# A two-block layer on one core: three norms split into halves, the residual into quarters, the last FFN tiles ahead of the last down blocks

## The reference, cut to what matters

```python
x = x + 0.5 * rmsnorm(swiglu(rmsnorm(x, ffn1_pre_g), w_gu, w_down), ffn1_post_g)
h = rmsnorm(x, mix_pre_g); ...                      # attention + state space, then w_mix_out
x = x + rmsnorm(mixed, mix_post_g)
qx = rmsnorm(x, xa_pre_g) @ xa_w_q                  # norm 3 of the kernel
kx, vx = split(rmsnorm(mem, mem_norm_g) @ xa_w_kv)  # norm 1
x = x + rmsnorm(softmax(qx kx) vx @ xa_w_o, xa_post_g)
x = x + 0.5 * rmsnorm(swiglu(rmsnorm(x, ffn2_pre_g), ...), ffn2_post_g)   # norm 4
proj = rms_norm(x, g_norm_2) @ w_in_2; ...          # norm 5, second block
```

## Time and profile before

| | |
|---|---|
| median of 3 runs | 1121.4 us (1121.01 to 1122.61) |
| the profiled execution | 1121.69 us, of which the span is 1119.9 us |
| PE busy | 1104.4 us, 99% of the span, 8484 matmul records |
| DVE busy | 793.0 us, 71% |
| ACT busy | 590.9 us, 53% |
| DMA | 188.59 MB, mean 168 GB/s |

### The profile page before, as it was taken

One profiled execution on the slowest core, in us unless ns is written; L12 is line 12 of the kernel. 1 busy time (PEld: TensorE's weight loads), 2 busy tenths in 40 slices (PEclk: granted clock), 3 DMA queues, 4 the chain that ended last, 5 costly groups with the idle time before them and its releaser, 6 DMA issues.

```text
span 1119.9 us, 20894 instructions
## 1 busy us (share of the span) xinstructions
PE 1104.4 (99%) x8484; PEld 1042.5 (93%) x8484; DVE 793.0 (71%) x1112; ACT 590.9 (53%) x844; POOL 0.2 (0%) x4
## 2 busy tenths in 40 slices
PE   9999999999999999999999999999999999999998
PEld 8999999999999999999999898999999799999998
DVE  5755555858898977777777867665555686987774
ACT  5444444557664325586744555443443575664561
POOL 0000000000000000000000000000000000000000
PEclk9999999999999999999999999999999999999999
DMA  8665555455544236444555434355555345543341
GB/s 298 241 222 187 190 184 188 168 183 180 185 151 148 94 136 207 155 147 151 188 174 177 169 114 160 131 200 206 173 176 206 128 166 198 184 151 114 114 151 38
DMA packets 29137, 188.59 MB, mean 168 GB/s; under 512 B 3496, under 2 KB 4809, under 8 KB 7370
## 3 DMA queue, kind: packets, MB, share of 16 engines
q1 hardware_dynamic: 26592, 181.42, 46.8%
q10 hardware_dynamic: 2474, 6.15, 1.7%
HBM read 186.50 MB, written 1.05 MB: 167 GB/s over the span
## 4 chain that ended last, share of the span: by engine, by line
PE 79%; DVE 15%; ACT 4%; issue 2%; DVEq 0%; ACTq 0%
PE bank L500 23%; PE bank L502 23%; PE bank L501 23%; DVE sb_w_lo L1973 4%; PE bank L581 2%; DVE sb_ssd_conv L2196 1%; ACT sb_w_hi L1287 1%; PE bank L816 1%; PE bank L961 1%; PE bank L655 1%; PE bank L1033 0%; PE bank L1012 0%; DVE sb_ssd_xdt L2243 0%; DVE sb_hyF L2626 0%; DVE sb_hyF L2625 0%
## 5 line engine op out<-in xcount | busy, mean ns | idle before, releaser
L1973 DVE TENSOR_TENSOR sb_w_lo<-sb_w_raw,sb_w_hi 128x2048 fp32r<-128x2048 f32 x169 | 386.5, 2290 | 156.9 <-ACT sb_w_hi L1287 156.7
L500 PE MATMUL bank<-sb_hT_hi,sb_w_hi 128*128 128x256 f32 x1560 | 442.7, 284 | 1.4 <-DVE sb_hT_lo L2050 1.3
L502 PE MATMUL bank<-sb_hT_hi,sb_w_lo 128*128 128x256 f32 x1560 | 435.3, 279 | 0.0
L501 PE MATMUL bank<-sb_hT_lo,sb_w_hi 128*128 128x256 f32 x1560 | 435.2, 279 | 0.0
L1287 ACT ACTIVATE sb_w_hi<-sb_w_raw 128x2048 fp32r<-128x2048 f32 x169 | 322.4, 1908 | 36.3 <-PE bank L502 34.9
L500 PEld LDWEIGHTS bank<-sb_hT_hi,sb_w_hi 128*128 128x128 f32 x1560 | 292.2, 187 | 6.0 <-issue 3.6
L501 PEld LDWEIGHTS bank<-sb_hT_lo,sb_w_hi 128*128 128x128 f32 x1560 | 291.8, 187 | 2.4 <-issue 1.2
L502 PEld LDWEIGHTS bank<-sb_hT_hi,sb_w_lo 128*128 128x128 f32 x1560 | 292.3, 187 | 0.0
L1341 ACT ACTIVATE sb_ffn_gate<-sb_ffn_gate 128x256 f32<-128x256 f32 x44 | 18.4, 418 | 140.7 <-DVE sb_ffn_gate L2065 140.7
L500 PE MATMUL bank<-sb_w_hi,sb_hT_hi 128*128 128x256 f32 x256 | 73.2, 286 | 0.6 <-DVE sb_hT_lo L2725 0.3
L501 PE MATMUL bank<-sb_w_lo,sb_hT_hi 128*128 128x256 f32 x256 | 71.1, 278 | 0.0
(11 more groups left out here) (431 smaller groups left out, 1751.3 us busy)
## 6 DMA issues: line engine op xcount, KB each, us to landing
sb_w_raw<-in_w SPq DMA_DIRECT2D x169, 1024.0 KB, 5.0
sb_x<-in_x SPq DMA_DIRECT2D x2, 512.0 KB, 4.6
sb_w_raw<-in_w SPq DMA_DIRECT2D x4, 256.0 KB, 7.0
sb_w_raw<-in_w SPq DMA_DIRECT2D x2, 512.0 KB, 8.2
sb_mem_xn<-in_mem ACTq DMA_DIRECT2D x1, 1024.0 KB, 7.8
sb_post_g<-in_ffn_post_g ACTq DMA_DIRECT2D x2, 512.0 KB, 4.6
sb_decay<-in_c_decay ACTq DMA_DIRECT2D x1, 768.0 KB, 4.3
out<-sb_x SPq DMA_DIRECT2D x3, 256.0 KB, 2.2
```

Of the source, the lines that this page charges most:

```text
L500: pe.matmul(o, a_hi, b_hi, start=first, stop=False)
L501: pe.matmul(o, a_hi, b_lo, start=False, stop=False)
L502: return pe.matmul(o, a_lo, b_hi, start=False, stop=last)
L1973: tt(w_lo[b % STAGES][:], w_raw[b % RING][:], f32(w_hi[b % STAGES][:]), ALU.subtract).then_inc(w_lo_in, 1)
```

## The change

Six edits.

1. **Norms 3, 4 and 5 in halves.** `raw_turn` transposes only columns 0 to 511 of x (banks 3, 4) ahead of the first block; the other eight transposes stand inside that block, in front of k = 4. The block (`raw_feature`, `raw_token`) has its two output tiles in two banks (7 and b % 3) and runs all products with the high halves of x first (k = 0 to 7, four each), then those with the low halves (two per k).
2. **Residual in quarters.** x is added to in four instructions, both token tiles of columns 0 to 511 first; the last post-gain scaling stands just ahead of the fourth, and the root no longer waits for it.
3. **Conversions moved behind the norm on ACT.** `after(mix_out + 3)` (block 100) stands behind the high halves of norm 3 and the last two tap copies; `after(xa_o + 3)` stands behind the high halves of norm 4 and the squares.
4. **End of an FFN.** up 20, up 21, [norm 1], down 9, down 10. Tiles 20 and 21 have halves of their own (`last_hi`, `last_lo`). In the last down block the bank is the outer loop. One `w_hi` and one `w_lo` move with it.
5. **Spectrum banks**: 3, 4, 1, 2 and 7, 1, 2, 0 in place of 3 to 6 and 0, 1, 2, 7.
6. **Second block**: `hyena_product(0, 1)` moves from i = 1 to the end of i = 0, ahead of a `w_lo`.

```diff
     def ffn(n):
         for j in range(FF_TILES):
-            if j % 2 and j > 1:
+            if j % 2 and 1 < j < FF_TILES - 1:
                 add(f"ffn{n}", f"ffn{n}_w_down", [(0, D)], 2, (j - 3) * P)
             add(f"ffn{n}", f"ffn{n}_w_gu", [(j * P, P), (D_FF + j * P, P)])
+        add(f"ffn{n}", f"ffn{n}_w_down", [(0, D)], 2, (FF_TILES - 4) * P)
         add(f"ffn{n}", f"ffn{n}_w_down", [(0, D)], 2, (FF_TILES - 2) * P)
...
+            def raw_turn(n, i_post, half):
+                for t in range(TOK):
+                    for k in range(4 * half, 4 * half + 4):
+                        if t == 0 and k % 2 == 0:
+                            claim(f"norm{n}.{k // 2}", 3 + k // 2)
+                        if k % 4 == 0:
+                            pe.wait_ge(S("x_ready"), X_READY[i_post] - 3 + 2 * half + t)
...
+            def raw_feature(key, b, n, i_post, a_hi, a_lo):
+                hi, lo = weights(b, KD, 256)
+                o = raw_blocks(key, b)
+                for k in range(KD):
+                    if k == 4:
+                        raw_turn(n, i_post, 1)
+                    high_there(n, k)
+                    for i in range(2):
+                        c = slice(i * P, (i + 1) * P)
+                        pe.matmul(o[i][:, 0:SEQ], hi[:, k, c], a_hi[:, k, :], start=k == 0, stop=False)
+                        pe.matmul(o[i][:, 0:SEQ], lo[:, k, c], a_hi[:, k, :], start=False, stop=False)
+                for k in range(KD):
+                    low_there(n, k)
+                    for i in range(2):
+                        mm = pe.matmul(o[i][:, 0:SEQ], hi[:, k, i * P:(i + 1) * P], a_lo[:, k, :], start=False, stop=k == KD - 1)
...
                 up_block(FF_TILES - 2)
-                down_block(PAIRS - 2)
                 up_block(FF_TILES - 1)
                 if n == 1:
                     norm_turn(1, mem_xn, 1, (7, 0, 2, 1))
-                down_block(PAIRS - 1)
+                down_block(PAIRS - 2)
+                last_down()
...
-                after(FIRST[stage] + 3)
...
             for i in range(6, 8):
                 taps(i)
+            after(FIRST["mix_out"] + 3)
             post_gain(2, POST[2])
...
-                for t, c in ((0, slice(0, D)), (1, slice(0, D // 2)), (1, slice(D // 2, D))):
-                    stt(x[:, t, c], y[:, t, c], rstd[:, 2 + t:3 + t], x[:, t, c], ALU.mult, ALU.add).then_inc(S("x_ready"), 1)
+                for half in range(2):
+                    c = slice(half * 512, (half + 1) * 512)
+                    for t in range(TOK):
+                        if half and t:
+                            scale_last()
+                            wait_read(dve, keys[-1])
+                        stt(x[:, t, c], y[:, t, c], rstd[:, 2 + t:3 + t], x[:, t, c], ALU.mult, ALU.add)\
+                            .then_inc(S("x_ready"), 1)
```

More of the change, by code:

```diff
@@ L598, in raw_turn @@
                         if t:
[L599 to L610, removed]
+                            ends(mm, f"norm0.{i}")
+            def raw_turn(n, i_post, half):
[5 more added lines that the diff above has]
+                            pe.wait_ge(S("x_ready"), X_READY[i_post] - 3 + 2 * half + t)
+                        c = k % 2 * SEQ + t * P
+                        mm = turn(banks[3 + k // 2][:, c:c + P], x[:, t, k * P:(k + 1) * P])
+                        if t and k % 2:
+                            ends(mm, f"norm{n}.{k // 2}")
@@ L1731, in _ @@
                 o = full(act, f"xaq{i}")
-                copy(f"xaq{i}", xa_q[:, 2 * i:2 * i + 2, :], two(o))
+                if i == 0:
+                    copy("xaq0", xa_q[:, 1, :], o[:, 0:SEQ])
+                    o = full(act, "xaq0.0")
+                    copy("xaq0.0", xa_q[:, 0, :], o[:, 0:SEQ])
+                else:
+                    copy(f"xaq{i}", xa_q[:, 2 * i:2 * i + 2, :], two(o))
                 if i >= 3:
@@ L1776, in token_scale @@
                 return ins
-            o = full(act, "cq0")
             act.wait_ge(S("xn_ready"), 5)
-            read(token_scale(cq[:, :, 0:256], two(o)), "cq0")
+            for t, key in enumerate(("cq0.0", "cq0")):
+                o = full(act, key)
+                read(act.activation(cq[:, t, 0:256], o[:, 0:256], ACT.Copy, scale=xr[:, t:t + 1]), key)
             after(FIRST["cq"])
@@ L2105, in ffn_part, with scaled @@
                 dve.wait_ge(S("post_g_in"), 16 * (i_post + 1))
-                for i in (1, 0, 3, 2):
+                def scaled(i):
+                    dve.wait_ge(S("post_ssq"), POST_SSQ[i_post] - 3 + i)
                     t, h = i // 2, slice(i % 2 * 512, (i % 2 + 1) * 512)
-                    key = f"down{n}.{i}"
-                    o = full(dve, key)
-                    if i % 2 == 0:
-                        dve.wait_ge(S("post_ssq"), POST_SSQ[i_post] - 3 + i)
-                    read(stt(f["xn"][:, t, h], o[:], 0.5, post_g[:, h], ALU.mult, ALU.mult), key)
+                    o = banks[fills[f"down{n}.{i}"][0]]
+                    read(stt(f["xn"][:, t, h], o[:], 0.5, post_g[:, h], ALU.mult, ALU.mult), f"down{n}.{i}")
@@ L2115, in ffn_part, with residual @@
+                for i in range(3):
+                    scaled(i)
                 link(stt(post_sum[:], post_ssq[:, :, 0], 1.0 / D, post_eps[:], ALU.mult, ALU.add))
                 dve.wait_ge(S("post_ssq"), POST_SSQ[i_post])
-                residual(i_post, [f"down{n}.{i}" for i in range(4)], f["xn"], 1)
-            def residual(i_post, keys, y, last):
+                residual(i_post, [f"down{n}.{i}" for i in range(4)], f["xn"], 1, lambda: scaled(3))
+            def residual(i_post, keys, y, last, scale_last):
```

166 lines of the change are left out of this document (116 added, 50 removed).

## The result

| | before | changed |
|---|---|---|
| median | 1121.5 us (6 runs) | 1126.0 us (1124.41 to 1126.61, 6 runs) |
| ratio | 1 | 1.0036, 95% interval 1.0023 to 1.0049 |
| profiled execution | 1121.69, span 1119.9 | 1124.61, span 1122.8 |
| PE busy, matmul records | 1104.4, 8484 | 1105.5, 8484 |

Another six executions of the changed kernel gave 1125.06 (1123.80 to 1126.21), so a fair value is 1125.5. The forecast was 1123.1, in a range of 1120.2 to 1126.0: the sign was right, the size less than half of it, and the first median lies on the upper edge of the range.

A forecast was written before the change was run, and what follows sets the result against it. PE, busy 99% of the span, was taken as the bound, so only its idle time could change. Terms 4.9 - 1.3 - 1.1 + 0.6 - 1.4 = +1.7 gave 1123.4 us profiled, 1123.1 median, range 1120.2 to 1126.0.

The forecast's parts named there:

- Norm 3, +4.9: Block 100's late w_hi delays DVE's w_lo and the chain to head 0's softmax transposes; PE 4.9 us later.
- second rival: At xa_turn of head 0 the clock falls to half after the new wait, costing 1.8 us more: 1124.9; 15%.
- Norm 4, -1.3: Earlier root, x in quarters and free banks start norm 4's first block sooner; 1.3 us gained, between 0 and 2.0.
- stall before k = 4: In the first block of norms 3, 4 and 5, PE waits some 0.6 us for the second half's hT_hi.
- Norm 5, -1.1: Earlier root and half the turns gain 1.1 us (0 to 1.8); PE waits 0.7 at the sb_sec_xn transposes.
- End of FFN 1, +0.6: PE waits 0.95 us for bank 0 at norm 1's transposes, a 0.38 wait goes; 0.6 lost (0 to 1.1).
- Second block, -1.4: Spectra products fill DVE's idle time, head 1's maximum comes earlier, PE's 1.37 us wait goes; 1.4 gained.
- third rival: The second block's gain doesn't come, as later w_lo or ACT's exps keep PE waiting: 1124.5 us; 10%.
- first rival: The delay at norm 3 never reaches PE, so the other terms stand alone: 1118.7 us; 12%.
- edge of +4.6: Upper end of the forecast range, 1126.0 us: the clock's fall with one more gain gone.

The follow-up runs named there:

- early_hi: The changed kernel with ACT's w_hi of block 100 back ahead of the taps; 1122.1 us, ratio 1.001.
- before_late_hi: The kernel before with only ACT's w_hi of block 100 moved behind the last two tap copies; 1123.55 us, ratio 1.0021.
- reorder3: early_hi with DVE's w_lo of block 100 ahead of its low halves of x, and both engines' square sums between their halves; 1118.45 us, ratio 0.9973.
- busy_wait: The changed kernel with 18 extra 512-column matmuls on PE just ahead of the transposes of xa_p, results unread; 1122.74 us.
- bank_order: reorder3 with only norm 1's transposes in banks 7, 2, 1, 0 in place of 7, 0, 2, 1; 1117.78 us.
- late_product: reorder3 with the product of the spectra back at its old place behind the w_lo; 1119.87 us.
- whole_turns: reorder3 with all 16 transposes of norms 4 and 5 ahead of the first block, none inside it; 1116.2 us.
- combined: The changed kernel with early w_hi and w_lo of block 100, whole transposes at norms 3, 4, 5, norm 1's banks 7, 2, 1, 0; 1116.15 us, ratio 0.9952.

## Why the prediction was right in sign and short in size

- **Norm 3, +4.9.** Measured +4.9 (from 0.5 late to 5.35 late), with the wait of 4.4 to a tenth. The chain was right step by step: turns, `hT_hi`, tap copies, `w_hi`, and `w_lo` at 638.45 where 637.9 was forecast, with PE 0.5 late. What the prediction didn't say is how much of it is whose. It had DVE's low halves end "near 635.3", by which the halves alone would cost 2.3 (635.3 less 633.04) and the conversion 2.6. They end at 636.6, and block 100's `w_lo` stands behind them whatever ACT does: the halves alone cost 2.9 and the conversion 1.9 (early_hi, before_late_hi), and only reorder3 removes both. The expectation of early_hi makes the prediction say less than it did, when it gives it the theory that the conversion is the whole of the delay.
- **The clock.** This was the second rival, with 15%. The sum had the clock's fall at nothing, and that is the larger part of what it was short by; the rival's own time, 1124.9, lies near the second median. Its price, 1.8 from the earlier trace rows, measured 1.5 to 2.9 in the traces. The granted clock of 0.50 behind the wait shows it, and busy_wait shows that idleness was the cause. The rule of the Trainium skill ("TensorE: Matmul & The Clock Gate", section "Why this matters for your kernels"), that idle gaps between bursts of matmuls put the clock back to the half, agrees with the traces that have gaps of 4.44 and 2.96, where the clock was 0.50. It should have weighed more than the silence of a trace that held no such wait.
- **Norm 4, -1.3.** Measured -1.3, from the spectrum's first matmul to the root transposes (16.55 before, 15.24 changed). The stall before k = 4 was 0.35, not 0.6, here and at norms 3 and 5, and the first product came 1.7 behind the first transpose. The 0.7 won ahead of the spectrum was in no term.
- **Norm 5, -1.1.** Measured -1.1, with a wait of 0.45 at `sb_sec_xn` in place of 0.7.
- **End of FFN 1, +0.6.** The wait is 0.99 (0.95 predicted) and the shift behind it +0.9. bank_order confirms that it is lost for good, apart from chance.
- **Second block, -1.4.** Measured -1.6, and 1.4 by late_product. The third rival is refuted.
- The first rival, that nothing reaches PE, is refuted by the 4.4.

With the measured terms the sum is 0.9 + 4.9 + 2.3 - 1.3 - 1.1 - 1.6 = +4.1. The profiled pair has +2.9, which is, but for rounding, 0.7 less for the products ahead of norm 4, and 0.4 less between the state-space branch and norm 3, where PE waits 0.9 for ACT's `sb_ssd_xF` in the trace of before and 0.4 in that of the changed kernel. The same code has the one or the other in the traces of the experiments. The medians lie 3.7 to 4.5 apart, nearer to the +4.1.

The largest chance, 0.47, went to a time within 0.2% of before, and the kernel is 0.36% slower, which had 0.41. That 1126.0 lies in the range at all was luck in part. The edge of +4.6 was made of the clock's fall and one more gain gone. The clock did fall, but no gain was gone.

## What to carry to other kernels

Splitting work so that the matrix engine can start earlier also makes the last part later; ask what stands behind that last part on the other engines, and let the urgent instruction go into the hole that the split opens there. When a change makes one long idle gap on the matrix engine, price the gap and the half clock behind it, since the second can be half as large as the first. Look at the mean clock of every execution and not only at the one trace: the trace of early_hi was the one execution of eleven in which the clock held. Undo each part alone before keeping it: here the halves of the transposes gave nothing at norm 4, and cost 0.7 at norm 5 and, with both delays gone, 0.3 at norm 3. The kernels without them at norms 4 and 5 are the fastest but for chance.

## What the runs showed of the hardware

**Two paces of the same product.** Starts of successive 256-column products at full clock lie either 0.1135 or 0.1177 us apart, for a whole stretch between two interruptions, and the pace changes at interruptions. The share of products at the faster pace was 17% to 23% in the traces. Between kernels it changes in stretches with the same code: a run of 152 such products that ends at the spectrum of norm 4 took 17.2 us in whole_turns and 17.9 in combined and in the kernel before. Over the whole stretch from the transposes of head 2 to that spectrum, every one of the fourteen traces lies near 27.55 or near 28.25. A window of ten us in them, PE only (length, busy and count, clock, DMA share, GB/s), whole_turns:

```profile
680.00:690.00 10.00, 10.00 (x91) 1.00 0.29 96
```

and combined:

```profile
680.00:690.00 10.00, 10.00 (x87) 1.00 0.44 152
```

Both are busy throughout at full clock, with 91 and 87 matmuls. That the weight transfers slow the products is a rival; reorder3 speaks against it, with the slower pace at the lowest load of the three:

```profile
680.00:690.00 10.00, 10.00 (x87) 1.00 0.26 81
```

Over all starts of successive 256-column matmuls that lie 0.110 to 0.121 apart, some 6690 in each trace, the mean was 0.11679 in whole_turns, 0.11697 in reorder3 and 0.11701 in combined; 0.0002 on each is 1.3 us. That is the size of what the waits leave open: whole_turns' extra 1.3 and combined's missing gain. The two traces of the changed kernel differ by 0.00007 (0.11684 and 0.11677), which is 0.5 us, and have the same pace ahead of norm 4, so how far the program fixes it isn't shown. What selects the pace stays open, and as there is one trace for each comparison, that it explains the medians is argued and not shown.

**The half clock.** The granted clock was 0.50 behind waits of 4.44 and 2.96 us and full behind those of 2.50 (early_hi) and 1.62 (before_late_hi), one trace each. The mean clock of all executions corrects this: it is below 1.000 in twelve of twelve at 4.44, in seven of eleven at 2.96, in ten of eleven at 2.50 and in none of ten at 1.62. Where it fell in the executions without a trace isn't shown, and 5 of 61 of the kernel before, whose longest wait was 1.8, are below 1.000 too. How long the half clock lasts differs between executions of one program: some 6.8 and 3.4 us in the two traces of the changed kernel, at costs of 2.2 and 1.5.
